# Hybrid attention and ConvFFN trunk on 8 cores: normed rows enter the feature layout by a transposing DMA instead of TensorE transposes

## The chip, the cores and the metric

One Trainium2 chip, 8 cores, each running the same program on two of the sixteen sequences. The cores do not talk to each other. The metric is the device time of the slowest core in microseconds; three runs of the kernel before are shown, with their median.

## The reference

Each of two layers has a token mixer and a channel mixer, both with an RMS norm ahead and an RMS norm behind:

```
h = rms_norm(x, g_pre);  proj = h @ w_in                        # 1024 -> 5120: q, k, v of 16 heads, two gates
o_a = dilated windows (128,1), (512,4), (2048,16), 4 heads each; o_b = block-sparse attention, 4 heads
merged = sigmoid(gate_a) * (o_a @ w_br_dil) + sigmoid(gate_b) * (o_b @ w_br_moba)
x = x + rms_norm(merged @ w_out, g_post)

h = rms_norm(x, g_pre)
u = gelu(causal_dwconv3(h @ w_gate) + b) * (h @ w_up)           # 1024 -> 2816
x = x + rms_norm(u @ w_down, g_post)
```

x is (16, 2048, 1024) float32. Every product contracts over features, so the normed h must stand with features on the partitions, while a norm is taken over a row of a token, with tokens on the partitions. So h has to be transposed four times per sequence: twice in each of the two layers.

## The kernel before

**Layout.** A core's two sequences (s) run one after the other, and in each the two layers (l). `hT` holds the normed h of one sequence, features on partitions: 8 chunks of 128 features by 2048 tokens, bf16. It has 16 tiles of 128 tokens. x itself lives in DRAM (`xs`) between sublayers.

**Tails.** What ends a sublayer and makes the next `hT` is called a tail. It handles 8 token tiles (a half, `hf`), one unit per tile. `tail_out` (line 514) ends the mixer: 16 matmuls per unit against `w_out` (L537). `tail_down` (line 495) ends the FFN: 44 matmuls per unit against `w_down` (L1252). A unit then goes through stages:
- a1: ScalarE squares the 128x1024 product z out of PSUM and sums it (L418), GpSimd makes the scale (L403, L406);
- a2: VectorE scales z (L427), adds it to x (L433), SyncE stores x;
- b1: ScalarE squares and sums the new x (L458), GpSimd makes the next scale;
- b2: VectorE writes the normed row tile `hb` in bf16 (L467). This write is what the program calls `h_tok`;
- c: TensorE transposes the eight 128x128 blocks of `hb` into one PSUM bank (L487), and ScalarE copies the bank into `hT` (recorded at L368, 128x1024).

**Order.** Every engine has one instruction stream, written out by the order in which the Python code calls it. In `tail_down`, the matmuls of unit i are issued first; then stages b1, b2 and c of unit i-1, then a1 and a2 of unit i. So on TensorE the transposes of unit i-1 stand between the matmuls of units i and i+1, and on ScalarE the copy into `hT` of unit i-1 stands ahead of the square a1 of unit i. The transposes of the last unit are put on a list (`late`) and issued some 9.5 cost units into the work that follows (`pump`).

`tail_out(0)` runs merged with `gates(1)`, and `tail_out(1)` with the first gate and up products of the FFN (`gate_up`, L379), the two streams being interleaved by estimated costs that generators yield. `tail_down(0)` is followed by `gate_up` of the second half, `tail_down(1)` by `v_proj` of the next layer (L608), which reads the `hT` tiles one after another in sixteen steps.

The tails of the last layer of the first sequence norm rows of the next sequence's x in b1 and b2, and those of the last layer of the last sequence have no b and c stages. Beside the tails, 16 tiles are transposed at the start of the program, with copies by VectorE (L371).

**Rings.** `hb` has 3 slots, x tiles 4, weight slabs 8. GpSimd issues the weight loads, with a cast from float32 to bf16; SyncE issues x loads, x stores and small transfers.

Of the kernel before, what the change touches and what calls it, by code (L numbers as in the profile page):

```python
# [135 lines left out]
def build(n_seq=2, n_layers=2):  # L136
    nc = bass.Bass("TRN2", target_bir_lowering=False)
# [25 lines left out]
    es = contextlib.ExitStack()  # L163
    with es:
# [4 lines left out]
        ACT = Q(nc, es, nc.scalar, "act", attach=True)  # L169
        DVE = Q(nc, es, nc.vector, "dve", attach=True)  # L170
        POOL = Q(nc, es, nc.gpsimd, "pool")
        SP = Q(nc, es, nc.sync, "sp")

        def dma(q, out, in_, so, **kw):
            q.eng.dma_start(out=out, in_=in_, **kw).then_inc(so.sem, 16)  # L175
            so.n += 16
            return (so, so.n)

        hTb = sb("hT", [128, 8 * SEQ], BF16)
        hT = hTb[:, :].rearrange("p (c t) -> p c t", c=8)  # L180
# [9 lines left out]
        NX = 4  # L190
        xr = sb("xr", [128, NX, 1024], F32)
        tz = sb("tz", [128, 2, 1024], F32)
        NH = 3
        hb = sb("hb", [128, NH, 1024], BF16)
        NST = 4
        stat = sb("stat", [128, 2, NST, 3], F32)
# [38 lines left out]
        ALLB = BankSet(range(8))  # L235
# [3 lines left out]
        UB2 = BankSet([3, 4])  # L239
        FB2 = BankSet([5, 6, 7])  # L240
        ALL6 = BankSet([0, 1, 2, 3, 4, 5])
        FB3 = BankSet([3, 4, 5, 6, 7])
        TB3 = BankSet([2])
        TB_ = BankSet([6, 7])
        zi = [0]

# [11 lines left out]
        def z_pair(n=3):  # L258
            b = 2 * (zi[0] % n)
            zi[0] += 1  # L260
            for i in (b, b + 1):
                assert bank_free[i] is not None
                PE.wait(bank_free[i])
                bank_free[i] = None
            return b
# [113 lines left out]
                inst = nc.tensor.matmul(out, lhsT=l_, rhs=r_, start=(i == 0), stop=(i == n - 1))  # L379
            return PE.do(inst)  # L380

        late = []

        def pump(cost):
            if late:
                late[0][0] -= cost
                if late[0][0] <= 0:
                    late.pop(0)[1]()

        def flush_late():  # L390
            while late:
                late.pop(0)[1]()

        hT_tok = [None] * 16
        hslot = [0]
        hfree = [[] for _ in range(NH)]
        stslot = [0]
        tslot = [0]
# [9 lines left out]
        def stage_a1(u):  # L408
            zb = u["zb"]
            z = psum[:, 512 * zb:512 * zb + 1024]  # L410
            hs = hslot[0] % NH
            hslot[0] += 1
# [65 lines left out]
        def stage_c(u, banks, q):  # L478
# [13 lines left out]
            bank_free[b] = [te]  # L492
            hT_tok[t] = te

        def tail_down(hf, zmm, mk, ahead):
            us = []
            nxt = {}
            recent = [ALLB.ids[(ALLB.i - 1 - k) % 8] for k in range(4)]
            zi[0] = min(range(3), key=lambda p: (2 * p in recent) + (2 * p + 1 in recent))

            def get_x(i):
                if i < 8 and i not in nxt:
                    nxt[i] = mk(hf * 8 + i)
            for i in range(8):
                for k in range(ahead + 1):
                    get_x(i + k)
                u = nxt.pop(i)
                u["zb"] = z_pair()
                u["z_tok"] = zmm(i, u["zb"])
                us.append(u)  # L510
                if i >= 1:
                    stage_b1(us[i - 1])
                    stage_b2(us[i - 1])
                    stage_c(us[i - 1], TB_, ACT)
                stage_a1(u)
                stage_a2(u)
                get_x(i + 1)
            stage_b1(us[7])
            stage_b2(us[7])
            zb = us[7]["zb"]  # L520
            ALLB.ids = [(zb + 2 + k) % 8 for k in range(8)]
            ALLB.i = 0
            if us[7]["nx"] is not None:
                late.append([9.5, lambda u=us[7]: stage_c(u, ALLB, ACT)])

        def tail_out(hf, mts, mk):
            us = [mk(hf * 8), mk(hf * 8 + 1)]
            mT = mTs[hf]
            for i in range(8):
                u = us[i]  # L530
                zb = z_pair(1)
                u["zb"] = zb
                PE.wait(mts, st["wout_tok"])
                inst = None
                for n in range(2):
                    for kc in range(8):
                        inst = nc.tensor.matmul(ps[zb + n], lhsT=mT[:, kc, i * 128:(i + 1) * 128], rhs=wout_t[:, kc, n * 512:(n + 1) * 512],  # L537
                                                start=(kc == 0), stop=(kc == 7))
                u["z_tok"] = PE.do(inst)
                stage_a1(u)  # L540
                yield 3.6
                if i >= 1:
                    stage_c(us[i - 1], TB3, ACT)
                stage_a2(u)
                if i + 2 < 8:
                    us.append(mk(hf * 8 + i + 2))
                yield 2.6
                stage_b1(u)
                yield 2.6
                stage_b2(u)  # L550
                yield 2.6
            yield 2.0
            stage_c(us[7], TB3, ACT)

        VOFF = (0, 64, 192, 256)
        A_U = 52 * KB
# [31 lines left out]
        def v_proj(l, G, banks, toks, waits):  # L588
            V = Vb[G]
            t_ones = ones_memset(V, waits)  # L590
            c0 = 12 + 2 * G if G < 3 else 22
            b0, t0, s0 = load_w(l, c0)
            b1, t1, s1 = load_w(l, c0 + 1)
            assert s1 == s0 + 1
            d = DILS[G] if G < 3 else 1
            L = SEQ // d
            tp = None
            for tau in range(16):
                r = (128 * tau) // L
                i0 = (128 * tau) % L  # L600
                start = i0 * d + r
                b = banks.get()
                PE.wait(t0, t1, [hT_tok[i] for i in range(start // 128, (start + 127 * d) // 128 + 1)])
                inst = None
                for kc in range(8):
                    w0 = b0[:, kc * 128:(kc + 1) * 128]
                    rhs = bass.AP(tensor=w0.tensor, offset=w0.offset, ap=[list(w0.ap[0]), [1024, 2], [1, 128]])
                    inst = nc.tensor.matmul(ps[b][:, 0:256], lhsT=hT[:, kc, start:start + 127 * d + 1:d],  # L608
                                            rhs=rhs, start=(kc == 0), stop=(kc == 7))
                tp = PE.do(inst)  # L610
                q = evac_eng()
                q.wait(tp, waits)
                v6 = V[:, tau, :].rearrange("p (a b c) -> p a b c", a=2, c=64)
                tc_ = copy_on(q, v6[:, :, 0:3:2, :], ps[b][:, 0:256].rearrange("p (a b c) -> p a b c", a=2, c=64))
                bank_free[b] = [tc_]
                toks.append(tc_)
                if tau == 0:
                    toks.append(t_ones)
                pump(0.9)
                yield 0.9  # L620
            slab_ring.release(s0, tp)
            slab_ring.release(s1, tp)

        def proj_fm(l, ci, banks, consume):
            buf, tokw, s = load_w(l, ci)
            tp = None
            for tg in range(4):
                b = banks.get()
                tp = mm_group(ps[b], [(buf[:, kc * 128:(kc + 1) * 128], hT[:, kc, tg * 512:(tg + 1) * 512]) for kc in range(8)],
                              [tokw, hT_tok[4 * tg:4 * tg + 4]])  # L630
                bank_free[b] = consume(tg, b, tp)
                pump(1.75)
                yield 1.75
            slab_ring.release(s, tp)

# [343 lines left out]
        def gates(l, hf, oa_toks, ob_done, banks, waits, toks, wload):  # L979
            abf = st.setdefault("ab_free", [[], [], [], []])  # L980
            mT = mTs[hf]
            for oc in range(8):
# [5 lines left out]
                for tgi in range(2):  # L988
# [7 lines left out]
                    ACT.wait(t_ga, abf[ia], waits)  # L996
                    s1 = ACT.do(nc.scalar.activation(out=A_, in_=ps[b_ga], func=AF.Tanh, scale=0.5))
                    bank_free[b_ga] = [s1]
                    pump(1.75)
                    yield 1.75  # L1000
                    b_gb = banks.get()
                    t_gb = mm_group(ps[b_gb], [(bgb[:, kc * 128:(kc + 1) * 128], hT[:, kc, tsl]) for kc in range(8)], [tgb])
                    ACT.wait(t_gb, abf[ia + 1])
                    s2 = ACT.do(nc.scalar.activation(out=B_, in_=ps[b_gb], func=AF.Tanh, scale=0.5))
                    bank_free[b_gb] = [s2]
                    pump(1.75)
                    yield 1.75
                    b_ya = banks.get()
                    t_ya = mm_group(ps[b_ya], [(bwa[:, kc * 128:(kc + 1) * 128], oaT[:, kc, tsl]) for kc in range(2)], [twa, oa_toks])
# [25 lines left out]
        def mixer(s, l, xs_tok, p_wait, pre):  # L1035
# [2 lines left out]
            ures = {}  # L1038
            if pre is None:
                drain(v_proj(l, 0, ALLB, vt[0], p_wait))  # L1040
                flush_late()
                qt[(0, 0)] = []
                drain(qk_proj(l, 0, 0, QK[0], p_wait, qt[(0, 0)], ALLB))
            else:
                vt[0], qt[(0, 0)] = pre
# [104 lines left out]
        def ffn(s, l, xs_tok, rest, r_free):  # L1150
# [3 lines left out]
            for hf in range(2):  # L1154
                wtok = {}

                def stage1(i, fc, tgi):
# [3 lines left out]
                    if tgi == 0:  # L1161
                        cur["g"] = slab_ring.load((l, "g", fc))
                        cur["u"] = slab_ring.load((l, "u", fc))
                        if hf == 0:
                            if fc == 0:
                                POOL.wait(r_free)
                            if fc == 14:
# [6 lines left out]
                    b_a = fb[0].get()  # L1174
                    t_a = mm_group(ps[b_a], [(bg[:, kc * 128:(kc + 1) * 128], hT[:, kc, tsl]) for kc in range(8)],
                                   [tg_w, hT_tok[4 * tg:4 * tg + 4]])
                    pump(1.75)
                    yield 1.75
                    b_u = fb[0].get()
                    t_u = mm_group(ps[b_u], [(bu[:, kc * 128:(kc + 1) * 128], hT[:, kc, tsl]) for kc in range(8)], [tu_w])  # L1180
                    pump(1.75)
                    if tgi == 1:
                        slab_ring.release(sg, t_u)
                        slab_ring.release(su, t_u)
# [38 lines left out]
                ut = {}  # L1223
                fb = [FB3 if hf == 0 else ALLB]

# [12 lines left out]
                    merge(gate_up(), rest_all(), 1.4)  # L1238
                else:
                    drain(gate_up())  # L1240
                flush_late()
                if hf == 1:
                    DVE.wait(st.get("halo_tok"))
                    tz_ = DVE.do(nc.vector.memset(halo[:, :, :], 0.0))
# [11 lines left out]
                us = []  # L1256
# [31 lines left out]
        PE.wait(ID)  # L1288
        vt0, qt0, tq = [], [], []
        v0 = v_proj(0, 0, ALL6, vt0, [])  # L1290
        late_c = []

        def qk_tg():
            gens = [qk_one(0, 0, 0, w, QK[0], [], qt0, ALL6) for w in range(2)]
# [9 lines left out]
        for t in range(16 + 2):  # L1304
            if t < 16:
                u = {"t": t, "nx": x0[t]}
# [28 lines left out]
        for s in range(n_seq):  # L1335
# [3 lines left out]
                ffn(s, l, xs_tok, rest, r_free)  # L1339
                p_wait = st["ut_free"] + [st["u1_tok"]]  # L1340
            outs += xs_tok
        flush_late()
        for q in (PE, ACT, DVE, SP):
            q.wait(outs)
            q.flush()
# [101 lines left out]
```

How the kernel before makes its waits and increments, by code:

```python
    def wait(self, *toks):  # L49
        acc = {}
        self._collect(toks, acc)
        for so, v in acc.items():
            if self.seen.get(so, 0) >= v:
                continue
            self.seen[so] = v
            if self.pending is not None:
                self.eng.wait_ge(self.pending[0].sem, self.pending[1])
                self.pending = None
            if self.attach:
                self.pending = (so, v)
            else:
                self.eng.wait_ge(so.sem, v)
# [1 line left out]
    def flush(self):  # L64
        if self.pending is not None:
            self.eng.wait_ge(self.pending[0].sem, self.pending[1])
            self.pending = None
# [1 line left out]
    def do(self, inst):  # L69
        if self.pending is not None:
            inst._wait_ge(self.pending[0].sem, self.pending[1])
            self.pending = None
        inst.then_inc(self.so.sem, 1)
        self.so.n += 1
        return (self.so, self.so.n)
# [98 lines left out]
        def dma(q, out, in_, so, **kw):  # L174
            q.eng.dma_start(out=out, in_=in_, **kw).then_inc(so.sem, 16)
            so.n += 16
            return (so, so.n)
```

## Time and profile before

| | |
|---|---|
| median of 3 runs (lowest to highest) | 3966.84 us (3966.76 to 4445.93) |
| the profiled execution | 3966.89 us, span of its slowest core 3965.6 us |
| cores | spans 3959.4 to 3965.6 us, granted clock 0.992 to 0.994 |
| TensorE matmul | 3821.5 us busy, 96% |
| VectorE | 2079.8 us, 52% |
| ScalarE | 1868.8 us, 47% |
| GpSimd | 876.1 us, 22% |
| DMA, mean over the span | 96 GB/s |

Busy time is the union of an engine's instructions. Matmuls are pipelined: one is recorded with some 379 ns while a new one starts every 216 ns, so costs on TensorE are read from start to start. A share of the span says little by itself; what counts is which engine ends the wait in the stretch that the change touches.

### The profile page before, as it was taken

How to read it: one execution, taken by the hardware profiler on the slowest of the kernel's cores; microseconds unless marked ns; L12 is line 12 of the kernel's file. 1: busy time of each engine (PE TensorE's matmuls, PEld its weight loads, DVE VectorE, ACT ScalarE, POOL GpSimd, SP SyncE). 2: the span in 40 equal slices, each digit the busy share in tenths (PEclk: the TensorE clock that was granted, in tenths of full speed). 3: DMA queues.
4: the chain of work that ended last, by engine and by line, in shares of the span. 5: the costliest groups of instructions: out<-in, count | busy, mean ns of one | idle time of the engine just before them, and what ended most of it. 6: DMA issues, size and time to landing. Idle time of an engine off the chain costs nothing.

```text
span 3965.6 us, 57672 instructions; the slowest of 8 cores (3959.4 to 3965.6 us)
## 1 busy us (share of the span) xinstructions
PE 3821.5 (96%) x20656; PEld 1859.7 (47%) x20656; DVE 2079.8 (52%) x3265; ACT 1868.8 (47%) x3653; POOL 876.1 (22%) x1484
## 2 busy tenths in 40 slices
PE   6989999999998999999999899999999989999999
PEld 4544444444554444444465344444446534444444
DVE  4454566455346456636435645664643564565363
ACT  3456355354345635535434554553533465465251
POOL 2331232111132133211113213221111322222110
PEclk9999999999999999999999999999999999999999
DMA  6132668344213367745432246783432225567341
GB/s 144 28 72 51 138 148 153 93 92 84 65 33 63 54 141 151 143 138 91 102 91 40 56 72 134 159 144 101 75 85 49 52 47 92 135 145 132 108 73 69
DMA packets 185600, 381.09 MB, mean 96 GB/s; under 512 B 32288, under 2 KB 48928, under 8 KB 185312
## 3 DMA queue, kind: packets, MB, share of 16 engines
q0 software_dynamic: 118656, 190.89, 31.3%
q1 hardware_dynamic: 66672, 186.51, 14.5%
q8 instruction: 178, 2.92, 0.3%
q14 instruction: 94, 0.77, 0.1%
HBM read 500.52 MB, written 67.63 MB: 143 GB/s over the span
## 4 chain that ended last, share of the span: by engine, by line
PE 90%; DVE 5%; ACT 3%; issue 1%; POOL 0%; DMA 0%; SPq 0%; DVEq 0%; POOLq 0%; ACTq 0%
PE psum L379 54%; PE psum L1252 15%; PE psum L537 6%; PE psum L608 5%; PE psum L660 5%; PE psum L939 3%; PE psum L685 2%; PE psum L487 1%; ACT s_arena L947 1%; DVE s_arena L781 1%; DVE s_arena L698 1%; DVE s_arena L371 0%; DVE s_hb L467 0%; ACT s_hb L458 0%; DMA s_xr<-x 0%
## 5 line engine op out<-in xcount | busy, mean ns | idle before, releaser
L379 PE MATMUL psum<-s_hT,s_slabs 128*128 128x512 bf16 x9728 | 2187.3, 379 | 7.5 <-DVE s_arena L1212 2.1
L379 PEld LDWEIGHTS psum<-s_hT,s_slabs 128*128 128x128 bf16 x9728 | 937.0, 98 | 1095.2 <-issue 25.3
L1252 PE MATMUL psum<-s_arena 128*128 128x512 bf16 x2816 | 615.0, 379 | 0.0
L1201 DVE SCALAR_TENSOR_TENSOR s_arena<-s_arena,s_convw 128x512 f32<-128x512 f32 x352 | 264.2, 751 | 434.8 <-ACT s_arena L1193 434.4
L1252 PEld LDWEIGHTS psum<-s_arena 128*128 128x128 bf16 x2816 | 274.1, 98 | 323.6
L660 PE MATMUL psum<-s_arena 128*128 128x128 bf16 (+2 forms) x1840 | 354.3, 268 | 63.3 <-DVE s_arena L951 21.2
L427 DVE SCALAR_TENSOR_TENSOR s_tz<-psum,s_stat,s_gpost 128x1024 f32<-128x1024 f32 x128 | 164.1, 1282 | 421.3 <-POOL s_stat L406 421.3
L947 ACT ACTIVATE s_arena<-psum 128x512 bf16<-128x512 f32 (+3 forms) x640 | 296.4, 550 | 72.3 <-PE psum L939 60.5
L175 POOL DMA_DIRECT2D s_slabs<-w_in_r x224 | 122.6, 550 | 908.1 <-PE psum L660 454.0
L698 DVE TENSOR_TENSOR s_arena<-s_arena,s_dmask 128x512 bf16<-128x512 bf16 (+1 forms) x384 | 192.1, 504 | 218.3 <-ACT s_arena L693 216.7
L1192 ACT COPY s_arena<-psum 128x512 f32<-128x512 f32 x352 | 205.6, 584 | 197.3 <-PE psum L379 197.3
L418 ACT ACTIVATE s_hb<-psum 128x1024 bf16<-128x1024 f32 x128 | 131.4, 1027 | 350.4 <-PE psum L1252 179.6
L403 POOL TENSOR_SCALAR s_stat<-s_stat 128x1 f32<-128x1 f32 x256 | 60.9, 238 | 1063.3 <-ACT s_hb L418 620.1
L693 ACT ACTIVATE s_arena<-psum 128x512 bf16<-128x512 f32 (+1 forms) x384 | 191.0, 506 | 199.6 <-PE psum L685 199.6
L1193 ACT ACTIVATE s_arena<-psum,s_convw 128x512 f32<-128x512 f32 x352 | 277.2, 787 | 0.0
L1204 DVE SCALAR_TENSOR_TENSOR s_arena<-s_arena,s_convw 128x512 f32<-128x512 f32 x352 | 264.7, 752 | 12.5
L175 POOL DMA_DIRECT2D s_slabs<-w_gate_r x176 | 97.5, 554 | 774.2 <-PE psum L379 761.5
L608 PE MATMUL psum<-s_slabs,s_hT 128*128 128x256 bf16 x2048 | 252.9, 277 | 6.3 <-DVE s_arena L371 5.6
L467 DVE SCALAR_TENSOR_TENSOR s_hb<-s_xr,s_stat,s_gpre 128x1024 bf16<-128x1024 f32 x128 | 164.3, 1284 | 178.4 <-POOL s_stat L406 169.7
L458 ACT ACTIVATE s_hb<-s_xr 128x1024 bf16<-128x1024 f32 x128 | 135.2, 1057 | 247.3 <-DVE s_xr L433 194.4
L1212 DVE TENSOR_TENSOR s_arena<-s_arena,psum 128x512 bf16<-128x512 f32 x352 | 239.6, 681 | 3.6 <-ACT s_arena L1210 3.6
L939 PE MATMUL psum<-s_arena 128*128 128x512 bf16 (+3 forms) x640 | 224.8, 360 | 7.7 <-ACT s_arena L947 4.9
(72 smaller groups left out, 3522.6 us busy)
## 6 DMA issues: line engine op xcount, KB each, us to landing
s_slabs<-w_in_r POOLq DMA_DIRECT2D x224, 256.0 KB, 4.5
xs<-s_xr SPq DMA_DIRECT2D x96, 512.0 KB, 3.5
s_xr<-xs SPq DMA_DIRECT2D x96, 512.0 KB, 4.6
s_slabs<-w_gate_r POOLq DMA_DIRECT2D x176, 256.0 KB, 3.9
s_slabs<-w_up_r POOLq DMA_DIRECT2D x176, 256.0 KB, 4.8
s_xr<-x SPq DMA_DIRECT2D x64, 512.0 KB, 5.6
s_arena<-w_down POOLq DMA_DIRECT2D x88, 256.0 KB, 6.0
y<-s_xr SPq DMA_DIRECT2D x32, 512.0 KB, 3.0
```

What stands on the lines that cost most here:

```text
L379: inst = nc.tensor.matmul(out, lhsT=l_, rhs=r_, start=(i == 0), stop=(i == n - 1))
L537: inst = nc.tensor.matmul(ps[zb + n], lhsT=mT[:, kc, i * 128:(i + 1) * 128], rhs=wout_t[:, kc, n * 512:(n + 1) * 512], start=(kc == 0), st ...
L608: inst = nc.tensor.matmul(ps[b][:, 0:256], lhsT=hT[:, kc, start:start + 127 * d + 1:d], rhs=rhs, start=(kc == 0), stop=(kc == 7))
L660: return nc.tensor.matmul(out, lhsT=V[:, tile, VOFF[hd]:VOFF[hd] + 128], rhs=rhs, start=start, stop=stop)
L698: ptoks[kt] = DVE.do(nc.vector.tensor_tensor(out=Pd[sl][:, :, 0:nq], in0=Pd[sl][:, :, 0:nq], in1=dmask[:, head:head + 2, 0:nq], op=ALU.mult))
L939: tS = PE.do(nc.tensor.matmul(ps[bS][:, 0:nq], lhsT=Kx[:, kt * 128:(kt + 1) * 128], rhs=Qx[:, qg * 512 + c0:(qg + 1) * 512], start=True, s ...
L947: tE = ACT.do(nc.scalar.activation(out=Pm[sl][:, 0:nq], in_=ps[bS][:, 0:nq], func=AF.Exp))
L1193: tt1 = ACT.do(nc.scalar.activation(out=t1_, in_=ps[b_a], func=AF.Identity, bias=convw[:, l, fc, 3:4], scale=convw[:, l, fc, 2:3]))
L1201: d1 = DVE.do(nc.vector.scalar_tensor_tensor(out=t1_, in0=a_[:, 1 + 512 * tgi:513 + 512 * tgi], scalar=convw[:, l, fc, 1:2], in1=t1_, op0= ...
L1204: d2 = DVE.do(nc.vector.scalar_tensor_tensor(out=t1_, in0=a_[:, 512 * tgi:512 + 512 * tgi], scalar=convw[:, l, fc, 0:1], in1=t1_, op0=ALU. ...
L1212: u1 = DVE.do(nc.vector.tensor_tensor(out=uT[:, u["fc"], u["tsl"]], in0=u["t1"], in1=ps[u["b_u"]], op=ALU.mult))
L1252: inst = nc.tensor.matmul(ps[zb + n], lhsT=uT[:, kc, i * 128:(i + 1) * 128], rhs=wdn[kc][:, n * 512:(n + 1) * 512], start=(kc == 0), stop= ...
```

## The change

All tail units (not the 16 tiles at the start) get their c stage from a transposing DMA that SyncE issues: it reads the `hb` slot and writes the tile of `hT` directly, with no PSUM bank, no TensorE instruction and no ScalarE copy. The `hb` ring grows from 3 to 4 slots, each with a semaphore for its DMA. The bank that `tail_out` kept for transposes joins the six-bank set of its companion work; `tail_down` rotates over four pairs of banks instead of three. The list `late` and its pump go away. In `tail_out` the c stage of a unit now comes right behind its b2 instead of in the next unit.

```diff
+        def dma_tr(out, in_, so):
+            nc.sync.dma_start_transpose(out=out, in_=in_).then_inc(so.sem, 16)
+            so.n += 16
+            return (so, so.n)
...
-        NH = 3
+        NH = 4
...
-        FB3 = BankSet([3, 4, 5, 6, 7])
-        TB3 = BankSet([2])
+        FB3 = BankSet([2, 3, 4, 5, 6, 7])
...
+        ht_so = [SemObj(nc, es, f"ht{i}") for i in range(NH)]
...
+        def stage_c_dma(u):
+            if u["nx"] is None:
+                return
+            hs, t = u["hs"], u["t"]
+            SP.wait(u["h_tok"])
+            te = dma_tr(hT[:, :, t * 128:(t + 1) * 128], hb[:, hs, :], ht_so[hs])
+            hfree[hs] = [te]
+            hT_tok[t] = te
...
-                u["zb"] = z_pair()
+                u["zb"] = z_pair(4)
...
                     stage_b2(us[i - 1])
-                    stage_c(us[i - 1], TB_, ACT)
+                    stage_c_dma(us[i - 1])
...
             stage_b2(us[7])
+            stage_c_dma(us[7])
...
-            if us[7]["nx"] is not None:
-                late.append([9.5, lambda u=us[7]: stage_c(u, ALLB, ACT)])
...
-                if i >= 1:
-                    stage_c(us[i - 1], TB3, ACT)
...
                 stage_b2(u)
+                stage_c_dma(u)
                 yield 2.6
-            yield 2.0
-            stage_c(us[7], TB3, ACT)
```

## Rows read from the trace of the kernel before

**Rows 1.** The page: engines' busy time, the chain that ended last by engine.
```profile
PE 3821.5 (96%) x20656; PEld 1859.7 (47%) x20656; DVE 2079.8 (52%) x3265; ACT 1868.8 (47%) x3653; POOL 876.1 (22%) x1484
PE 90%; DVE 5%; ACT 3%; issue 1%; POOL 0%; DMA 0%; SPq 0%; DVEq 0%; POOLq 0%; ACTq 0%
```

**Rows 2.** L487 from 100 us on: ns min/median/max; idle before it; copies into hT.
```profile
L487 PE MATMUL psum<-s_identb,s_hb x896: 216/219/219, 448.6 to 3568.8; 128*128 128x128 bf16 x180
  DVE s_hb L467: 6.0, 4
...
L368 ACT COPY s_hT<-psum 128x1024 bf16<-128x1024 bf16 x112 | 113.3, 1012 | 196.9 <-PE psum L487 196.8
```

**Rows 3.** Timeline of TensorE, tail_down: start, duration in us, idle before in brackets.
```profile
716.97 19.16 PE L1252 MATMUL psum<-s_arena 128*128 128x512 bf16 x88
...
736.41 9.66 PE L1252 MATMUL psum<-s_arena 128*128 128x512 bf16 x44
746.17 0.61 PE L487 MATMUL psum<-s_identb,s_hb 128*128 128x128 bf16 x8
746.61 9.66 PE L1252 MATMUL psum<-s_arena 128*128 128x512 bf16 x44
...
799.08 10.52 PE L379 MATMUL psum<-s_hT,s_slabs 128*128 128x512 bf16 x48 [1.30 <-ACT s_hT L368]
```

**Rows 4.** Chain of waits, last tail_down (no b, no c): start, duration.
```profile
3881.53 75.99 PE psum L1252 x352
```

**Rows 5.** Timeline of all engines, tail_down: one unit between two groups of transposes.
```profile
726.66 1.02 ACT L418 ACTIVATE s_hb<-psum 128x1024 bf16<-128x1024 f32 x1 [7.72 <-PE psum L1252]
...
746.81 1.01 ACT L368 COPY s_hT<-psum 128x1024 bf16<-128x1024 bf16 x1 [3.29 <-PE psum L487]
747.72 1.03 ACT L418 ACTIVATE s_hb<-psum 128x1024 bf16<-128x1024 f32 x1
...
754.94 1.28 DVE L467 SCALAR_TENSOR_TENSOR s_hb<-s_xr,s_stat,s_gpre 128x1024 bf16<-128x1024 f32 x1 [2.40 <-POOL s_stat L406]
```

**Rows 6.** Timeline of TensorE, tail_out(0) merged with gates(1).
```profile
521.59 0.61 PE L487 MATMUL psum<-s_identb,s_hb 128*128 128x128 bf16 x8 [1.51 <-DVE s_hb L467]
...
533.25 1.89 PE L379 MATMUL psum<-s_hT,s_slabs 128*128 128x512 bf16 x8
```

**Rows 7.** Timeline of all engines, from tail_down(1) into the next layer's v_proj.
```profile
1021.92 9.66 PE L1252 MATMUL psum<-s_arena 128*128 128x512 bf16 x44
...
1032.12 7.15 PE L608 MATMUL psum<-s_slabs,s_hT 128*128 128x256 bf16 x64
...
1033.22 1.03 ACT L418 ACTIVATE s_hb<-psum 128x1024 bf16<-128x1024 f32 x1
...
1042.21 1.91 PE L608 MATMUL psum<-s_slabs,s_hT 128*128 128x256 bf16 x16 [1.55 <-DVE s_arena L371]
```

**Rows 8.** Timeline, tail_down whose b stages norm the next sequence's x.
```profile
1782.26 1.03 ACT L418 ACTIVATE s_hb<-psum 128x1024 bf16<-128x1024 f32 x1
...
1788.15 1.28 DVE L467 SCALAR_TENSOR_TENSOR s_hb<-s_xr,s_stat,s_gpre 128x1024 bf16<-128x1024 f32 x1 [1.07 <-POOL s_stat L406]
```

**Rows 9.** DMA issues: KB each, median us from issue to landing.
```profile
s_arena<-qaug_t SPq DMA_DIRECT2D x16, 256.0 KB, 5.2
...
s_identb<-identb SPq DMA_DIRECT2D x1, 32.0 KB, 2.3
```

**Rows 10.** DMA queue of the weight loads: packets, MB, share of 16 engines.
```profile
q0 software_dynamic: 118656, 190.89, 31.3%
```

**Rows 11.** Windows: us, busy by engine, granted clock, DMA share, GB/s.
```profile
433.00:522.00 89.00, 87.44 (x452) 41.45 (x453) 54.81 (x64) 39.95 (x66) 28.08 (x58) 1.00 0.62 139
535.00:633.00 98.00, 97.75 (x500) 46.10 (x500) 67.41 (x81) 60.12 (x116) 29.40 (x63) 1.00 0.73 149
633.00:717.00 84.00, 84.00 (x391) 38.08 (x390) 51.35 (x75) 47.20 (x101) 19.14 (x36) 1.00 0.84 154
717.00:799.00 82.00, 80.19 (x409) 37.15 (x407) 29.08 (x25) 23.50 (x38) 11.41 (x30) 1.00 0.26 84
```

More of the change, by code:

```diff
@@ L380, in mm_group @@
             return PE.do(inst)
[L382 to L392, printed above, removed]
         hT_tok = [None] * 16
         hslot = [0]
+        ht_so = [SemObj(nc, es, f"ht{i}") for i in range(NH)]
         hfree = [[] for _ in range(NH)]
@@ L498, in tail_down @@
             recent = [ALLB.ids[(ALLB.i - 1 - k) % 8] for k in range(4)]
-            zi[0] = min(range(3), key=lambda p: (2 * p in recent) + (2 * p + 1 in recent))
+            zi[0] = min(range(4), key=lambda p: (2 * p in recent) + (2 * p + 1 in recent))
             def get_x(i):
@@ L618, in v_proj @@
                     toks.append(t_ones)
-                pump(0.9)
                 yield 0.9
@@ L631, in proj_fm @@
                 bank_free[b] = consume(tg, b, tp)
-                pump(1.75)
                 yield 1.75
@@ L998, in gates @@
                     bank_free[b_ga] = [s1]
-                    pump(1.75)
                     yield 1.75
@@ L1005, in gates @@
                     bank_free[b_gb] = [s2]
-                    pump(1.75)
                     yield 1.75
@@ L1040, in mixer @@
                 drain(v_proj(l, 0, ALLB, vt[0], p_wait))
-                flush_late()
                 qt[(0, 0)] = []
@@ L1176, in stage1 @@
                                    [tg_w, hT_tok[4 * tg:4 * tg + 4]])
-                    pump(1.75)
                     yield 1.75
@@ L1180, in stage1 @@
                     t_u = mm_group(ps[b_u], [(bu[:, kc * 128:(kc + 1) * 128], hT[:, kc, tsl]) for kc in range(8)], [tu_w])
-                    pump(1.75)
                     if tgi == 1:
@@ L1240, in ffn @@
                     drain(gate_up())
-                flush_late()
                 if hf == 1:
@@ L1290, in build @@
         v0 = v_proj(0, 0, ALL6, vt0, [])
-        late_c = []
         def qk_tg():
@@ L1341, in build @@
             outs += xs_tok
-        flush_late()
         for q in (PE, ACT, DVE, SP):
```

## The prediction

> **What bounds the kernel now.** Start with the busy times and the chain that ended last [rows 1]: TensorE is busy 96% of the span and carries 90% of the chain. So the kernel is a TensorE stream with small holes, and an edit is worth what it takes out of that stream plus the holes that it closes. The granted clock is full, 1.00, in the four stretches that matter here [rows 11], so TensorE's time is a count of columns and nothing else.
>
> Next comes the line of the transposes [rows 2]. 896 instructions from 100 us on are 112 tail units of 8; the 16 tiles at the start stay as they are. That count is also the code's: 64 units of tail_out (2 sequences, 2 layers, 16 tiles) and 48 of tail_down (the last layer of the last sequence has none). They waited for VectorE's write of the normed rows 4 times, 6.0 us in total. ScalarE spends 1.01 us on each copy into hT.
>
> Last, the timeline around a tail_down unit [rows 3]. Eight transposes start at 746.17 and the next matmul at 746.61: a c stage takes about 0.445 us of TensorE, not the 1.75 us that eight durations of 219 ns add up to, because they are pipelined.
>
> **What the change takes out, step by step.**
>
> (1) The transposes: 112 x 0.445 = **49.8 us**. In both kinds of tail TensorE is the engine that everything else follows: 87.4 of 89 us and 97.8 of 98 us busy in the two tail_out stretches, 80.2 of 82 in tail_down [rows 11]. So all of it is on the path.
>
> (2) The loop through the copy. In tail_down one unit lasts 746.61 - 736.41 = 10.20 us [rows 3]. Its 44 matmuls take 75.99/8 = 9.50 us, from the tail without b and c stages [rows 4]. 10.20 - 9.50 - 0.445 leaves 0.255 us of idle time per unit. Where it comes from is seen in the next timeline [rows 5]: the square a1 of a unit starts at 747.72, only when ScalarE has finished the previous unit's copy (746.81 plus its duration), and the unit's normed rows are done at 754.94 + 1.28 = 756.22, 8.5 us after a1 began. Transposes, copy and a1-to-b2 together are a ring of 10.2 us, longer than 9.5 us of matmuls. Without c on TensorE and ScalarE the ring is cut: a1 starts about 0.2 us behind z (the first unit's matmuls end at 716.97 + 9.50 = 726.47, its a1 starts at 726.66 [rows 3, 5]), normed rows come 8.7 us after z, and TensorE waits for none of that. In the two-norm tails there are 6 such waits per tail (the first two units stand back to back, 88 matmuls in a row), 4 such tails: 24 x 0.255 = **6.1 us**. In the two tails of the first sequence's last layer, whose normed rows come from another x, I find no such wait: nothing is counted.
>
> (3) Once, TensorE waited 1.30 us for a bank that ScalarE's copy held [rows 3]: **1.3 us**.
>
> (4) The end of tail_out(0): the last transposes waited 1.51 us for the normed rows [rows 6], four times [rows 2]: **6.0 us**.
>
> (5) The seam from tail_down(1) into v_proj, two times (the two-norm tails). z of the last unit ends at 1021.92 + 9.50 = 1031.42; the tenth v_proj step starts at 1042.21, 10.79 us later, held up by an evacuation that queues on VectorE behind the last b2 [rows 7]. This step is tied to the last a1: 1042.21 - 1033.22 = 8.99 us. With a1 0.2 us behind z it starts at 9.2 us. Of the 1.59 us gained, 0.70 is in (1) and (2) already; 2 x 0.9 = **1.8 us**. What is late next is that same evacuation, so the rest of the hole stays.
>
> Sum of the gains: 49.8 + 6.1 + 1.3 + 6.0 + 1.8 = **65.0 us**.
>
> **What the change adds and moves.** 112 transposing DMAs of 256 KB on SyncE's queue, and as many waits there for h_tok. Behind each wait stand the store of the next unit's x and a load of x. Both need work that VectorE does after h_tok in any case (b2 of unit i-1 stands ahead of a2 of unit i), and loads are issued up to two units ahead, so the wait itself delays nobody: 0 us as long as SyncE isn't held by the DMA before it. The extra slot of hb gives a DMA three to four units (30 us and more) before a1 would want the slot. The x ring is not touched. The wider bank sets cost nothing. POOL's queue is moved past nothing.
>
> The trace of before has no transposing DMA, so I bound it twice.
>
> *Landing time T.* Lowest: the one 32 KB load of 128x128 bf16 took 2.3 us. Highest: eight such blocks one after another, 18.4 us. Nearest in size, type and queue is the 256 KB load of bf16 rows with 5.2 us [rows 9]; I take 5.2. Who waits for it? In tail_out(0) the last tile's rows are ready before 521.59, and the FFN starts at about 533.25 with tiles 0 to 3 [rows 6]: hidden up to 12 us and more. tail_out(1) and tail_down(0) feed work that comes a whole stage later. Only the last tile of tail_down(1) is urgent: v_proj's sixteenth step needs it. A step lasts 7.15/8, about 0.87 us from start to start [rows 7]; the tenth starts 9.2 us after z, so the sixteenth at 14.4; the rows are ready at 8.7. Slack 5.7 us. At the seam between sequences, a1 to the end of b2 is 1788.15 + 1.28 - 1782.26 = 7.2 us [rows 8], and fifteen steps are 13.0 us: slack 13.0 - 7.4 = 5.6. So T = 5.2 costs 0, and otherwise 3 x (T - 5.6): 38 us at 18.4.
>
> *Engine time e*, what all 16 DMA engines spend on one. Lowest: like x traffic. Tail_down moved 84 GB/s at a share of 0.26 [rows 11], which is 323 GB/s while busy, or 0.8 us for 256 KB. Highest: one packet for each of the 128 x 8 pieces of 256 bytes. The weight queue paid 0.313 x 3965.6 us / 118656 = 10.5 ns of all 16 engines per packet [rows 10]; 1024 packets make 10.7 us. I take 1 us, because bytes in and out are those of a plain copy of bf16 rows. The free share of the engines covers 1 us: tail_out(0) leaves 0.38 x 89 = 34 us for its eight, tail_out(1) and the gate_up behind it 182 - 0.73 x 98 - 0.84 x 84 = 40 us for theirs.
>
> The pages bear on T. In the Trainium skill, VectorE: DVE Perf Modes, section The three transpose paths, puts a 128x128 bf16 block at 1309 ns by DMA against 390 ns on TensorE, and its rules say to use TensorE where a PSUM destination will do. TensorE's price in rows 2 and 3 is far below that: 0.445 us for eight, in a stream. By the page's DMA price eight blocks would be an estimated 10.5 us, which costs 3 x 4.9 = 15 us at the seams and makes the time 3917 us. On the other side, Advanced Engine Details and Errata, section X-Bar Transpose, says that on this chip transposing DMAs are as fast as regular ones; no run here shows either yet.
>
> **The sum.** 3966.9 (the profiled execution; the median is 3966.8, so nothing shifts) - 65.0 = **3902 us**, 1.6% faster. The gain can't reach 2%, or 79 us, unless something outside the tails moves.
>
> **The rivals.**
>
> *A, late last tile or freed time lost.* T is 10 to 18 us, and v_proj stalls three times, or the DMAs queue up one behind another so that the eighth lands several us later still. By the bounds: 3902 + 13 to 38 = 3915 to 3940. The same is reached if the tail_out gain (64 x 0.445 + 6.0 = 34.5 us) goes into other waits of the merged streams: 3937. Against it: no engine but TensorE is over 69% busy there [rows 11], and the slack of 5.6 us has little room for error, which speaks for it.
>
> *B, slower: the DMA engines fill up.* While tail_out runs, the weight stream already takes 0.62 to 0.84 of them. Free are 34/8 = 4.2 us per transposing DMA in tail_out(0), 40/8 = 5 us in tail_out(1) with its gate_up, and (76 - 21)/8 = 6.9 us in tail_down. Beyond that the weights or x come late and TensorE waits. At e = 10.7: 8 x 6.5 and 8 x 5.7 per layer, four times, are 390 us, and 6 x 8 x 3.8 = 182 us in the tail_downs: 3902 + 572 = 4474. It decides from e of about 4.2; at 5.6 the gain of 65 us is gone; above about 6.9 the kernel is more than 2% slower. Against it: that needs transposed bytes to be seven times as dear as plain ones. For it: the trace has no row that excludes this.
>
> *C, over 2% faster.* A gain outside the tails, from the ScalarE relief or six banks; 3885. The holes of TensorE in the tails are all counted above, and I see none left.
>
> **Chances.** Forecast 0.70; A 0.16; B 0.12, of which 0.10 ends over 2% slower (about what a measurement of this kernel can tell from no change) and 0.02 between; C 0.02. Within 2%: 0.70 + 0.16 + 0.02 = 0.88. The forecast's own range is 3894 to 3915: 8 us for a wider set of banks and a lighter ScalarE, which I took as nothing, and 13 us for T at 10. The whole range, 3893 to 3948, goes on through A, with the same 8 us on top; B's upper part and C stay out.
>
> **What would show it.** L487 left with 128 instructions at the start and the 128x1024 copies of ScalarE gone; tail_down units of 9.50 us from start to start and 76 us for eight; no wait at the end of tail_out(0); the tenth v_proj step about 9.2 us after the last z, and the sixteenth without a wait for a DMA. The prediction is wrong if the landing of the new DMAs is over 5.6 us (A), if the DMA share in the tail_out stretches goes to 0.9 and more with TensorE waiting for slabs (B), or if SyncE's issue of one takes microseconds and x loads come late behind it.

## The result and the profile after

| | before | after |
|---|---|---|
| time of the slowest core | 3966.8 us | 3903.2 and 3906.2 us |
| ratio, 95% interval | | 0.984 [0.9823, 0.9857] |
| spans of the cores, profiled execution | 3959.4 to 3965.6 | 3892.4 to 3904.9 |

3902 was forecast, 3903.2 and 3906.2 came, 1.6% faster. (The median over all six executions, 4158.9 us, is no measure: in several of them one die ran at a lower clock, as it also does in some executions of the kernel before.)

The page's busy times, the chain by engine and the DMA queues of the changed kernel, slowest core (core 3):

```profile
PE 3765.8 (96%) x19760; PEld 1810.6 (46%) x19760; DVE 2078.2 (53%) x3265; ACT 1762.5 (45%) x3541; POOL 877.7 (22%) x1484
...
PE 91%; DVE 4%; ACT 2%; DMA 1%; issue 1%; POOL 0%; SPq 0%; ACTq 0%; POOLq 0%; DVEq 0%
...
q0 software_dynamic: 118656, 190.89, 33.3%
q1 hardware_dynamic: 184944, 215.88, 21.6%
```

TensorE has 896 instructions fewer, ScalarE 112, and VectorE's busy time hasn't moved [rows 1]. What is left of the transposes is the start of the program. The new line stands on SyncE. These are the line's own rows: instructions with ns min/median/max, and the landing of the DMAs, minimum, median, maximum in us:

```profile
L480 PE MATMUL psum<-s_identb,s_hb x128: 216/219/314, 16.4 to 74.2; 128*128 128x128 bf16 x128
...
L175 SPq DMA_TRANSPOSE s_hT<-s_hb x112: 1217/1218/12191, 442.0 to 3509.1; - x112
...
DMA to landing us min/median/max: 3.1/4.8/30.1
```

A tail_down on core 5, as the chain of waits has it (start, us): 352 matmuls in one piece where [rows 3] had transposes and waits between groups of 44.

```profile
706.90 75.97 PE psum L1242 x352
782.88 151.95 PE psum L383 x704
934.83 75.99 PE psum L1242 x352
...
1019.98 6.27 PE psum L606 x56
```

**Where the time came from.** The chain of waits gives the start of each stage. Laid side by side on core 5 (before 3965.6, after 3897.0 us), with what the steps of the prediction come to in each stage (the first row starts 128 matmuls ahead of tail_out(0), in gates(0); the fourth ends there):

| stages, summed over their instances | before, us | after, us | gained | forecast |
|---|---|---|---|---|
| last 128 matmuls of gates(0), then tail_out(0), x4 | 130.65, 131.66, 130.65, 131.06 | 125.64 each | 21.5 | 20.3 |
| tail_out(1) with gate_up, x4 | 181.95, 183.41, 182.18, 181.95 | 178.00, 178.01, 182.47, 178.01 | 13.0 | 14.2 |
| tail_down(0) and gate_up, x4 | 234.50, 231.50, 233.04, 227.92 | 227.9 each | 15.3 | 15.0 |
| tail_down(1), seam, mixer up to those 128 matmuls, x3 | 435.51, 429.39, 431.63 | 425.27, 426.61, 427.40 | 17.3 | 15.5 |
| start of the program | 404.53 | 403.26 | 1.3 | 0 |

Core 5 is one of eight. In the mean over the cores the five rows gain 21.1, 12.6, 15.2, 14.9 and 1.0 us, and the span falls by 65.2 us, from 3962.2 to 3897.0.

One stage stands out: the third tail_out(1) lasts 182.47 us and gained nothing. All eight cores have such a stage, with 180.8 to 182.5 us on seven of them. TensorE's timeline there (core 5), and its granted clock around it (windows: us, busy by engine, granted clock, DMA share, GB/s):

```profile
2526.80 10.52 PE L383 MATMUL psum<-s_hT,s_slabs 128*128 128x512 bf16 x48
...
2539.94 5.30 PE L383 MATMUL psum<-s_hT,s_slabs 128*128 128x512 bf16 x16 [2.62 <-DVE s_arena L1203]
```

```profile
2526.00:2540.00 14.00, 11.38 (x54) 5.03 (x53) 12.78 (x17) 9.70 (x21) 4.47 (x9) 1.00 0.88 151
2540.00:2546.00 6.00, 6.00 (x21) 2.39 (x22) 1.80 (x3) 0.62 (x3) 1.59 (x3) 0.72 1.19 194
```

A wait of 2.62 us for a bank, and behind it a clock of 0.72 in the mean over 6 us, so for a part of them at the lower of its two levels (1.2 of 2.4 GHz): 16 matmuls take 5.30 us instead of 3.6. Together 4.5 us. The fall of the clock is no fixed part of it. Cores 4, 6 and 7 had the same wait of 2.62 us and kept the full clock; their stage lasted 180.8 us, so there the wait cost 2.8 us. Core 4 (a row of TensorE's timeline, then the window behind the wait):

```profile
2537.70 12.46 PE L383 MATMUL psum<-s_hT,s_slabs 128*128 128x512 bf16 x56 [2.62 <-DVE s_arena L1203]
...
2537.70:2543.70 6.00, 6.00 (x28) 2.74 (x29) 2.67 (x5) 1.88 (x4) 1.59 (x3) 1.00 1.12 202
```

Experiments 3 to 5 explain the wait.

The slowest core of that execution, core 3, has something more in the same stage. Its chain of waits:

```profile
2504.19 12.19 SPq L175
...
2516.47 1.18 SPq L180
...
2517.81 22.79 DMA s_xr<-x
...
2540.62 1.24 DVE s_xr L426
...
2547.67 12.50 PE psum L383 x47
```

SyncE was held for 12.19 us by one transposing DMA, the x load behind it went out late and then took 22.79 us to land, VectorE's add waited for it, and with it the bank that TensorE wanted: 8.9 us of waiting there instead of 2.62. The stage is 7.2 us longer than on core 5. That is the larger part of the 12.5 us by which the slowest core is above the fastest, against 6.2 before; the rest stands in the mixers. Core 2 was held even longer in its second tail_out(1), 13.18 us, and lost only 1 us by it. In the kernel before, and in experiment 1, no issue on any core held SyncE for more than 2.6 us.

### The profile page after: what moved, and what is told of

It reads as the page before. It is cut to its first block, busy times and chain, and to the rows that moved or that the text cites. A ratio compares the mean times of both kernels' runs of the same rounds, so it can differ in the third digit from the quotient of the medians.

```text
span 3904.9 us, 56082 instructions; the slowest of 8 cores (3892.4 to 3904.9 us)
## 1 busy us (share of the span) xinstructions
PE 3765.8 (96%) x19760; PEld 1810.6 (46%) x19760; DVE 2078.2 (53%) x3265; ACT 1762.5 (45%) x3541; POOL 877.7 (22%) x1484
## 3 DMA queue, kind: packets, MB, share of 16 engines
q1 hardware_dynamic: 184944, 215.88, 21.6%
## 4 chain that ended last, share of the span: by engine, by line
PE 91%; DVE 4%; ACT 2%; DMA 1%; issue 1%; POOL 0%; SPq 0%; ACTq 0%; POOLq 0%; DVEq 0%
PE psum L383 55%; PE psum L1242 16%; PE psum L538 5%; PE psum L606 5%; PE psum L656 5%; PE psum L935 3%; PE psum L681 2%; ACT s_arena L943 1%; DMA s_xr<-x 1%; DVE s_arena L777 1%; DVE s_arena L694 1%; DVE s_arena L375 1%; ACT s_tz L372 0%; SPq L175 0%; DVE s_hb L460 0%
## 5 line engine op out<-in xcount | busy, mean ns | idle before, releaser
L656 PE MATMUL psum<-s_arena 128*128 128x128 bf16 (+2 forms) x1840 | 354.3, 268 | 63.7 <-DVE s_arena L947 21.5
L451 ACT ACTIVATE s_hb<-s_xr 128x1024 bf16<-128x1024 f32 x128 | 135.2, 1056 | 301.7 <-DVE s_xr L426 249.0
L1195 DVE SCALAR_TENSOR_TENSOR s_arena<-s_arena,s_convw 128x512 f32<-128x512 f32 x352 | 264.7, 752 | 12.5
```

Of the source, the lines that this page charges most:

```text
L656: return nc.tensor.matmul(out, lhsT=V[:, tile, VOFF[hd]:VOFF[hd] + 128], rhs=rhs, start=start, stop=stop)
L1195: d2 = DVE.do(nc.vector.scalar_tensor_tensor(out=t1_, in0=a_[:, 512 * tgi:512 + 512 * tgi], scalar=convw[:, l, fc, 0:1], in1=t1_, op0=ALU. ...
```

## The experiments

**1. No c stage at all.** The changed kernel leaves out the transposing DMAs and, with them, every write of `hT` after the start of the program.

```diff
         def stage_c_dma(u):
...
-            SP.wait(u["h_tok"])
-            te = dma_tr(hT[:, :, t * 128:(t + 1) * 128], hb[:, hs, :], ht_so[hs])
-            hfree[hs] = [te]
-            hT_tok[t] = te
+            hfree[hs] = [u["h_tok"]]
+            hT_tok[t] = u["h_tok"]
```

> The changed kernel with the transposing DMAs of all tails left out: nothing writes hT after the start of the program, and TensorE waits for the normed rows instead. Theory 1 (the DMAs are hidden, the gain is TensorE's time and its holes): the same as the changed kernel within 5 us on an undisturbed core, 3892 to 3900, with every tail stage as long as with the DMAs; the 4.5 us lost in the gate and up stage of the second sequence's first layer stay, because they are a matter of the bank order. Theory 2 (the DMAs cost something that the trace doesn't show as a wait): 15 us and more faster, below 3885. In both, the cores' spans lie closer together than the 12.5 us of the changed kernel if the late x load of one core came from DMA queues that are full.

Measured: 3898.8 and 3900.4 us, spans 3890.3 to 3897.5. On core 5 the stages are 125.6, 178.01, 227.92, and 182.41 in the odd one: the same as with the DMAs to within 0.1 us, apart from the mixers. So 112 transposing DMAs cost the path nothing where they land in time, and theory 1 stands. The slowest core is 3 to 7 us below the changed kernel's, and the spread is 7.2 us, not 12.5. The intervals of the two kernels overlap (0.9829 [0.9786, 0.9871] here), so the times don't show that difference; what the DMAs cost is read from the trace, and it is the late x load on core 3.

**2. Only tail_down by DMA.**

```diff
-        FB3 = BankSet([2, 3, 4, 5, 6, 7])
+        FB3 = BankSet([3, 4, 5, 6, 7])
+        TB3 = BankSet([2])
...
                 yield 3.6
+                if i >= 1:
+                    stage_c(us[i - 1], TB3, ACT)
...
                 stage_b2(u)
-                stage_c_dma(u)
                 yield 2.6
+            yield 2.0
+            stage_c(us[7], TB3, ACT)
```

> Transposing DMAs in tail_down only; tail_out transposes on TensorE as before. Theory 1: 48 x 0.445 + 6.1 + 1.3 + 1.8 = 30.6 us off 3967, so 3936, with tail_down at 76.0 us for eight units and tail_out(0) unchanged at 102.1 us. Theory 2 (the two parts lean on each other, through ScalarE's relief or the banks): more than 8 us away from that.

Measured: 3936.8 to 3940.0 us, ratio 0.9929 [0.99, 0.9957], for 3936 forecast. tail_down with its gate_up is 227.92 us everywhere, tail_out(0) stays at 102.13 us. Its third tail_out(1) lasts 185.2 us, 3 us more than before. The bank order in the table of experiment 3 is the likely reason; no run tests it there.

**3. Only tail_out by DMA**, with the six-bank set; tail_down is that of the kernel before.

```diff
...
-        FB3 = BankSet([3, 4, 5, 6, 7])
-        TB3 = BankSet([2])
+        FB3 = BankSet([2, 3, 4, 5, 6, 7])
...
-                if i >= 1:
-                    stage_c(us[i - 1], TB3, ACT)
...
                 stage_b2(u)
+                stage_c_dma(u)
                 yield 2.6
-            yield 2.0
-            stage_c(us[7], TB3, ACT)
```

> Transposing DMAs in tail_out only, with the six-bank set; tail_down as before. Theory 1: 64 x 0.445 + 6.0 = 34.5 us off 3967, so 3932, up to 4.5 us more where the bank order collides at the end of tail_out(1); stage tail_out(0) 97.1 us, tail_down 10.20 us a unit. Theory 2 (full DMA engines in these stretches eat the gain): 3940 to 3960, TensorE waiting in the gate and up products.

Measured: 3952.0 us in the profiled execution, the shortest, and up to 3978.7 us; ratio 0.9981 [0.9957, 1.0005]. Of 34.5 us some 15 came at best, and by the ratio 7.5, which is not clear of no change. The numbers of theory 2, but not its cause. tail_out(0) is 97.12 us, as forecast; no wait on slabs to speak of; yet three of the four tail_out(1) stages last 186.1 us instead of 178.0. TensorE's timeline in one of them (core 5):

```profile
1582.68 8.80 PE L383 MATMUL psum<-s_hT,s_slabs 128*128 128x512 bf16 x40
...
1595.83 5.30 PE L383 MATMUL psum<-s_hT,s_slabs 128*128 128x512 bf16 x16 [4.35 <-DVE s_arena L1223]
1602.83 7.50 PE L383 MATMUL psum<-s_hT,s_slabs 128*128 128x512 bf16 x34 [1.70 <-DVE s_arena L1223]
```

L1223 is the last VectorE step of a gate and up pair, the one that frees the bank of the up product. The bank counters of the program tell the rest. When tail_out(1) runs out, the companion work changes from its own set FB3 to all eight banks (ALLB), and goes on wherever ALLB's counter stood after the last mixer:

| kernel | oldest bank of FB3 at each of the four changes | bank at which ALLB starts | stage, us |
|---|---|---|---|
| before | 6, 4, 7, 5 | 0, 5, 5, 5 | 181.95, 183.41, 182.18, 181.95 |
| after | 2, 2, 2, 2 | 0, 2, 4, 0 | 178.00, 178.01, 182.47, 178.01 |
| experiment 2 | 6, 4, 7, 5 | 0, 2, 4, 0 | 181.95, 183.30, 185.23, 181.95 |
| this one | 2, 2, 2, 2 | 0, 5, 5, 5 | 178.00, 186.06, 186.14, 186.14 |

A bank that is taken out of turn was filled later than the oldest, so the VectorE step that frees it ends later, and TensorE waits. With six banks, starting two past the oldest costs 4.5 us on core 5, three past it 8.1 us.

**4. The bank handoff**, on the changed kernel.

```diff
                     yield from rest
+                    ALLB.ids = [FB3.ids[(FB3.i + k) % 6] for k in range(6)] + [0, 1]
+                    ALLB.i = 0
                     fb[0] = ALLB
```

> The changed kernel, but where tail_out(1) ends, the eight-bank set starts with the six banks in the order in which the companion work has used them, then 0 and 1. Theory 1 (TensorE's 2.62 us wait and the lower clock behind it in the second sequence come from taking bank 4 while bank 2 is the oldest): that stage goes from 182.5 to 178.0 us on every core, all other stages unchanged, so 4.5 us less. Theory 2 (VectorE is simply late there, from late x or weights): the wait stays at 2 to 3 us.

Measured: 178.01 us in the third stage, all other tail stages unchanged; spans 3889.1 to 3895.0, times 3896.4 to 3903.4 us, ratio 0.983 [0.9802, 0.9859]. Theory 1. All eight cores have 178.0 us there. It is the fastest version of this study, by some 4 us that the intervals of the times don't separate and the trace does.

**5. The handoff on experiment 3.** The same two lines.

> Transposing DMAs in tail_out only, plus the bank handoff: the eight-bank set starts with the six banks oldest first. Theory 1 (of the 34.5 us that this half should bring, the 24.3 us that went missing are bank order: the set started at bank 5 while bank 2 was the oldest, three times, 8.1 us each): all four tail_out(1) stages at 178.0 us, the time 3924 to 3930. Theory 2 (VectorE is late there for another reason): three stages stay at 186 us and the time at 3952.

Measured: 3927.0 and 3927.8 us, ratio 0.9896 [0.9867, 0.9925]; all four tail_out(1) stages at 178.01 us (core 1). Theory 1: with experiment 3 this puts the 24.3 us of the three long stages on the bank order alone.

**6. Every transposing DMA twice.**

```diff
-        NH = 4
+        NH = 3
...
-            SP.wait(u["h_tok"])
+            SP.wait(u["h_tok"], sc_tok[0])
             te = dma_tr(hT[:, :, t * 128:(t + 1) * 128], hb[:, hs, :], ht_so[hs])
-            hfree[hs] = [te]
+            t2 = dma_tr(scr[:, :].rearrange("p (c t) -> p c t", c=8), hb[:, hs, :], sc_so[hs])
+            hfree[hs] = [te, t2]
+            sc_tok[0] = t2
             hT_tok[t] = te
```

> The changed kernel with every transposing DMA issued twice, the second one into a scratch tile that nobody reads (and three slots of hb instead of four, to make room). Theory 1 (a transposing DMA is hidden, with room): tail_down stays at 76.0 us, tail_out(0) at 97.1, on an undisturbed core within 5 us of the changed kernel; the DMA share in the tail_out(1) stretch, 0.86 to 0.98, goes to 1 and more, so late x loads come on more cores and cost the slowest 10 to 40 us. Theory 2 (rival B, the engines were close to full): the weights come late, TensorE waits for slabs, 4050 and more.

Measured: 3929.9 us at best, without an interval. In the profile cores 0 to 3, with a mean granted clock of 0.990 to 0.993, span 3893.9 to 3914.1 us. Core 3 ran the tails in 97.1, 178.0 and 227.9 us with twice the DMAs, apart from the third tail_out(1) with its bank order (182.9). Its windows over tail_out(0), tail_out(1) and the gate_up behind it:

```profile
431.80:525.00 93.20, 93.14 (x432) 41.90 (x429) 60.77 (x72) 35.65 (x63) 30.81 (x63) 1.00 0.93 179
525.00:610.00 85.00, 84.96 (x395) 38.53 (x395) 58.24 (x68) 47.15 (x97) 26.25 (x57) 1.00 1.06 206
610.00:700.00 90.00, 90.00 (x419) 40.78 (x418) 58.27 (x82) 50.90 (x109) 22.15 (x42) 1.00 1.03 160
```

TensorE is at work without a gap with a DMA share of 0.93 to 1.06 (packets are counted side by side, so the share can pass 1). So a core has room for twice the DMAs as long as nothing comes late; the slowest core paid some 27 us. This is theory 1 in the numbers, but the longest waits of cores 0 to 2, 3.6 to 4.2 us in their tail_out(1) stages, don't come from late x loads as I had expected. Their chain on core 1:

```profile
581.22 20.18 DMA s_scr<-s_hb
...
602.76 15.35 DMA s_scr<-s_hb
...
618.13 1.11 ACT s_hb L414 x2
```

Each DMA into the scratch tile waits for the one before it, and it keeps the `hb` slot that ScalarE's square of a later unit wants; there are three slots here instead of four. So a part of the 27 us belongs to this experiment's own ring. Rival B's sign is there in small: TensorE waited for weight slabs a few times, 3.53 us at the longest. Its price of 4 us and more of all engines per DMA isn't seen.

**7. Eight DMAs of 128x128 for each one.**

```diff
-            te = dma_tr(hT[:, :, t * 128:(t + 1) * 128], hb[:, hs, :], ht_so[hs])
+            for c in range(8):
+                te = dma_tr(hT[:, c, t * 128:(t + 1) * 128], hb[:, hs, c * 128:(c + 1) * 128], ht_so[hs])
```

> The changed kernel with each transposing DMA cut into eight of 128x128, on the same queue. Asks what SyncE's 1.22 us for one issue are made of. Theory 1 (they grow with the bytes): 0.2 us each, the time unchanged, landing of the last about 5 us. Theory 2 (a fixed cost each): 8 x 1.2 = 9.8 us of SyncE per unit, more than the 9.5 us of a tail_down unit, x loads and stores late behind them, some 20 to 60 us slower than the changed kernel. A block alone at 1.3 us of transfer, one after another, would land 10 us after the issue and stall the sixteenth v_proj step by some 5 us, twice.

Measured: 4030.0 us at best; there is no interval. Core 5, read here, spans 4032.8 us at a mean clock of 0.974, so a part of that is clock. The line, and what waited for it (second block: us in total, times, longest):

```profile
L175 SPq DMA_TRANSPOSE s_hT<-s_hb x896: 1083/1202/2993, 441.1 to 3652.2; - x180
...
DMA to landing us min/median/max: 2.2/3.9/11.1
```

```profile
PE psum L607 <- DMA s_hT<-s_hb: 40.9, 5, 8.8
PE psum L383 <- DMA s_hT<-s_hb: 25.3, 4, 8.7
```

L607 is v_proj. Theory 2: an issue takes SyncE 1.2 us whether it carries 256 KB or 32 KB, eight take 9.6, and now v_proj does stall, 8.8 us at the longest. It cost some 125 us, over twice what I had written. 66 us are these waits, some of the rest is the clock; how much is left open. By stages core 5 lost 65 us in the three stretches from tail_down(1) through the mixer, 64 us in the four tail_out(1) and 10 us in one tail_down(0) with its gate_up.

**8. The copy by VectorE, in tail_down of the kernel before.**

```diff
-                    stage_c(us[i - 1], TB_, ACT)
+                    stage_c(us[i - 1], TB_, DVE)
```

> The kernel before, with the copy into hT done by VectorE instead of ScalarE in tail_down, so that the square a1 of the next unit doesn't stand behind it. TensorE's transposes stay. Theory 1 (0.255 us of idle time per unit comes from the ring through ScalarE's copy): the copy now stands ahead of a2 on VectorE but takes 0.68 us instead of 1.01, and a1 runs beside it; tail_down units go from 10.20 to 9.95 us, 24 x 0.255 = 6 us off, 3961. Theory 2 (the idle time belongs to the transposes' own start, a weight load after a wait): units stay at 10.20 us, 3967.

Measured: 3956.5 to 3957.8 us, ratio 0.9972 [0.9959, 0.9984]. The chain in a tail_down (start, us), core 5:

```profile
968.08 9.50 PE psum L1252 x44
977.58 0.45 PE psum L487 x8
978.03 9.50 PE psum L1252 x44
```

9.945 us from unit to unit instead of 10.20: the idle 0.255 us is gone with all transposes still in place. Theory 1. It also brought some 4 us at the seams and elsewhere that I had not counted.

**9. The start of the program by DMA too** (with the handoff), and beside it **10. the changed kernel once more**.

```diff
             if 1 <= t <= 16:
-                stage_c(first[t - 1], TB_, DVE)
+                stage_c_dma(first[t - 1])
```

> The changed kernel with the bank handoff, and the 16 tiles at the start of the program by transposing DMA too (no TensorE transpose is left). Theory 1: TensorE gets 16 x 0.45, about 7 us, back, but these tiles are urgent: v_proj follows one tile behind, each DMA lands about 5 us after its rows are ready, and only the last one's delay stays: -7 + 5, within 5 us of the kernel with the handoff alone, 3890 to 3900. Theory 2 (every step of the start waits for its DMA): 10 us and more slower than that one, the first mark of the first mixer at 410 us instead of 400 to 404.

> The changed kernel itself once more, beside the one with the handoff and the DMAs at the start, to have them on one chip. Theory 1: the undisturbed cores at 3892 to 3898; the slowest core 3897 to 3905, since which core meets full DMA queues changes from execution to execution. Theory 2 (the late x load of one core is a fixed property of that core): core 3 is the slowest again, at 3905.

Measured: 3934.9 us at best (ratio 0.9921 [0.9879, 0.9964]) against 3901.2 for the changed kernel beside it (0.9838 [0.9795, 0.988]). The tails are those of experiment 4, 97.11, 178.01 and 227.92 us; the first mixer's mark stands at 438.6 us on core 2 instead of 400 to 407. Waits of TensorE in the first 100 us, core 2 (in the changed kernel 35.2 us there, for VectorE's normed rows):

```profile
PE psum L606 <- DMA s_hT<-s_hb: 64.5, 9, 24.7
```

SyncE's order shows why it is so much. With the DMAs in it (start, us), the loads of x stand behind them:

```profile
19.91 1.31 SPq L175 DMA_TRANSPOSE s_hT<-s_hb  x1
21.75 0.34 SPq L180 DMA_DIRECT2D s_xr<-x  x1
22.13 1.44 SPq L175 DMA_TRANSPOSE s_hT<-s_hb  x1
28.36 0.33 SPq L180 DMA_DIRECT2D s_xr<-x  x1
```

and in the changed kernel 14 of the 16 loads go out in one stretch, up to 49 us:

```profile
1.99 46.98 SPq L180 DMA_DIRECT2D s_xr<-x  x14
```

Here a load waits behind the wait for the rows of a tile, so each tile's delay is handed to the next, and TensorE, idle for so long, is granted a mean clock of 0.62 from 50 to 100 us (0.93 in the changed kernel). Theory 2, three times as dear as I had put it. Run 10 gave 3901.2, 3903.3 and 3905.4 us; in its profile core 2 is the slowest, 3904.1, not core 3, so theory 2 is out. But the slowest core is late for another reason this time: the tails of core 2 are as on the others (182.5 us in the third tail_out(1), as on core 5), and it lost its time at the start of the program (406.5 us, the others 401.2 to 406.2) and in the first mixer (429.7, the others 425.4 to 427.2). So what a late x load costs differs from execution to execution, and in this one it cost the slowest core nothing.

## Why the prediction was right, and where it was off

**(1) The transposes, 49.8 us: right.** The stages give it back one by one. tail_out(0) lost 5.01 us, which is 8 x 0.445 and the wait of 1.51 us of step (4) to within 0.1. Two of the tail_out(1) stages lost 3.95 us, for 3.56 forecast; tail_down(0) with its gate_up in the next-sequence tail lost 3.58.

**(2) The loop through the copy, 6.1 us: right, and shown twice.** By the units of 9.50 us after, and by experiment 8, which took away only the copy from ScalarE and lost the 0.255 us per unit.

**(3), (4) Right:** nothing waits there now; the last tail_out(0) unit ends without a gap.

**(5) The seam, 1.8 us: right in its mechanism.** z ends at 1010.8 on core 5 and the tenth step starts at 1019.98, 9.2 us later, as worked out, and it is still the same VectorE evacuation that holds it up (1.32 us). The stages around it agree only in their sum: forecast were 6.0, 3.6 and 6.0 us, core 5 gained 10.2, 2.8 and 4.2, the mean of eight cores 6.8, 3.4 and 4.7. Why the mixers behind a tail get shorter or longer by some us was not looked into.

**The landing time, 5.2 taken: 4.6 to 5.3 in the median of a core.** The urgent ones, the last tile of tail_down(1), landed in 3.1 to 4.8 us on all cores, inside the slack of 5.6 us: no core waited for a transposing DMA. The Trainium skill's 1309 ns a block (VectorE: DVE Perf Modes, The three transpose paths) would have made 10.5 us for eight, as an estimate; eight blocks in one DMA landed after 3.1 us at the least on this core, so here the price doesn't add up over blocks. One block alone took 2.2 us from its issue in experiment 7.

**The engine time, 1 us taken: mis-sized, without effect.** On core 5 the SyncE queue's share went from 14.5% of 3965.6 us to 20.2% of 3897.0: 212 us, or 1.9 us per DMA. With every DMA doubled it is 25.5% of 3893.9 us on core 3, 1.8 us for each further one. (On core 3 of the changed kernel, where the queues jammed, it was 2.4 us.) That queue has (184944 - 66672)/112 = 1056 packets more per DMA. So the upper bound's count of pieces was right and its price of 10.5 ns was not: 1.8 ns. The Trainium skill, Advanced Engine Details and Errata, section X-Bar Transpose, says that transposing DMAs are as fast as regular ones; in engine time they are not here, 1.9 us against an estimated 0.8 for the same bytes, while the landing (4.8 us; 5.2 for 256 KB before [rows 9]) agrees.

**What I called nothing and was not: the wider bank set.** "The wider bank sets cost nothing" is the step that failed. The set FB3 with six banks now ends every tail_out at the same oldest bank, 2, and the eight-bank set starts at 0, 2, 4 and 0: 4.5 us lost once, luckily once. Experiment 3 had 24 us of it. Against the 4.5 us stand gains that I had not counted, on core 5 1.3 us at the start, 1.2 us in the first row of the table, 3.3 us in the tail_out(1) stages (1.4 of them are the bank order of the second one before) and 1.8 us around the mixers. ScalarE's relief or the wider sets may be behind the rest; no run separates that.

**What was luck.** The mean span fell by 65.2 us where 65.0 were summed up, but one loss and several gains that the sum left out cancel in it: with the handoff of experiment 4 the mean span is 3891.6 us, 70.6 below the kernel before. The forecast is right by its mechanism; that it is right to 1 to 4 us is luck in part.

**"The wait itself delays nobody, as long as SyncE isn't held by the DMA before it."** It is held in single cores, where weights, x and transposes fill the DMA engines: 12.19 us, and core 3 paid 7.2 us for it. This is rival B in miniature, and it is most of the step from 68.6 us on core 5 to 60.7 us for the slowest core of the profiled execution. The other time, 3903.2 us, has no trace.

**Rival A** (late last tile) and **rival B** at its price didn't occur. Experiments 7 and 9 are what A looks like when it does. A's second form, freed time that goes into other waits, did come in experiment 3, by the bank order.

## What to carry to other kernels

Where one engine carries 90% of the chain, the worth of work taken off it is its start-to-start time, not its recorded durations, plus the rings that pass through the engine that helped it; both can be read off one unit of the timeline. Moving work to a DMA queue is free for consumers that come late and for loads that don't stand behind it: count slack for the one urgent tile, and look what else is in the issuing engine's order. When buffer sets are changed, check at every handover from one set to the next that the first buffer taken is the oldest one.

## What the runs showed of the hardware

- The issue of a transposing DMA holds SyncE for 1.2 us, for 32 KB as for 256 KB (1202 and 1218 ns in the median), some four times the 0.33 us of a plain one. On two cores, where the DMA engines were full (share 1.45 from 2504 to 2517 us on core 3), it was held up to 12.19 and 13.18 us, and a plain store among them 8.09 us.
- A 128x1024 bf16 tile lands in 3.1 us at best (medians 4.6 to 5.3), a 128x128 one in 2.2 (median 3.9).
- 1056 packets per 128x1024 tile, 1.8 ns of all 16 engines each, or 1.9 us per tile.
- A wait of 2.62 us of TensorE, which had been busy throughout, was followed on core 5 by a mean granted clock of 0.72 over 6 us and cost 4.5 us; on core 4 the same wait left the clock at 1.00 and cost 2.8 us. In experiment 3 waits of 4.35 and 1.70 us, with a mean clock of 0.83 over 10 us, cost 8.1 us.
